# A long block model on one Trainium2 core: reordering the first mixer's projection and the start of its recurrence

## The reference, cut to what matters

```python
def project(h):
    p = h @ w_in
    qkv = jax.nn.silu(depthwise_conv(p[..., :2 * GDN_KW + GDN_VW], conv_w))
    q = _l2norm(qkv[..., :GDN_KW]...)
    k = _l2norm(qkv[..., GDN_KW:2 * GDN_KW]...)
    v = qkv[..., 2 * GDN_KW:]...
...
decay = jnp.exp(jnp.where(tril, gcum[..., :, None] - gcum[..., None, :], -jnp.inf))
lower = jnp.where(strict, jnp.einsum('nbhid,nbhjd->nbhij', kb, kc) * decay, 0.0)
sol = lax.linalg.triangular_solve(eye + lower, rhs, left_side=True, lower=True, unit_diagonal=True)
attn = jnp.where(tril, jnp.einsum('nbhid,nbhjd->nbhij', qc, kc) * decay, 0.0)
...
def step(S, inp):
    v_new = u_i - w_i @ S
    o = (q_i * exp(g_i)) @ S + a_i @ v_new
    S = S * exp(g_last) + (k_i * exp(g_last - g_i)).T @ v_new
```

## Time and profile before

| what | us |
|---|---|
| median of 3 runs | 4353.49 (4348.59 to 4356.99) |
| profiled execution, its own time | 4360.86 |
| its span | 4359.1 |
| busy: TensorE | 3892.0 (89%) |
| busy: VectorE | 1823.6 (42%) |
| busy: ScalarE | 980.9 (23%) |
| busy: GpSimd | 377.2 (9%) |

### The profile page before, as it was taken

One profiled execution on the slowest core, in us unless ns is written; L12 is line 12 of the kernel. 1 busy time (PEld: TensorE's weight loads), 2 busy tenths in 40 slices (PEclk: granted clock), 3 DMA queues, 4 the chain that ended last, 5 costly groups with the idle time before them and its releaser, 6 DMA issues.

```text
span 4359.1 us, 49807 instructions
## 1 busy us (share of the span) xinstructions
PE 3892.0 (89%) x20860; PEld 2379.2 (55%) x20860; DVE 1823.6 (42%) x2818; ACT 980.9 (23%) x1915; POOL 377.2 (9%) x928
## 2 busy tenths in 40 slices
PE   7988898898899999789888989888888999998999
PEld 4577555785534434577766765222344433445777
DVE  2644445553302212368777441110236478115443
ACT  3411223222301111345554321000124200100000
POOL 0023001210100000000000000000040077000000
PEclk9989998999899999799998998999987999999999
DMA  5232122311298897121100426999911011231331
GB/s 189 87 97 57 52 97 70 101 64 35 102 380 340 342 382 303 61 78 59 68 30 30 122 83 255 421 421 421 338 60 59 20 34 49 77 101 58 99 95 58
DMA packets 278559, 631.24 MB, mean 145 GB/s; under 512 B 63552, under 2 KB 205376, under 8 KB 219456
## 3 DMA queue, kind: packets, MB, share of 16 engines
q1 hardware_dynamic: 275712, 627.40, 39.1%
q10 hardware_dynamic: 2624, 0.66, 0.1%
HBM read 611.75 MB, written 16.25 MB: 144 GB/s over the span
## 4 chain that ended last, share of the span: by engine, by line
PE 67%; DVE 11%; DMA 10%; ACT 4%; POOL 4%; issue 2%; SPq 2%; ACTq 0%; DVEq 0%; POOLq 0%
PE ps L1505 10%; PE ps L1792 10%; PE ps L1165 6%; PE ps L1511 4%; PE ps L1842 4%; DMA arena<-moe_w_down 4%; DMA arena<-moe_w_gate 2%; PE ps L1399 2%; PE ps L1411 2%; PE ps L1658 2%; PE ps L1654 2%; PE ps L1663 2%; DMA arena<-moe_w_up 2%; PE ps L1103 2%; PE ps L2009 1%
## 5 line engine op out<-in xcount | busy, mean ns | idle before, releaser
L1505 PE MATMUL ps<-arena 128*64 128x512 f32 x3072 | 707.7, 600 | 79.6 <-DMA arena<-moe_w_up 22.4
L1505 PEld LDWEIGHTS ps<-arena 128*64 128x64 f32 x3072 | 207.3, 137 | 528.2 <-issue 383.6
L1165 PE MATMUL ps<-arena 128*128 128x512 f32 (+1 forms) x768 | 251.3, 486 | 3.5 <-DVE g_rows L2731 2.1
L3054 DVE SCALAR_TENSOR_TENSOR arena<-arena,ps 128x512 f32<-128x512 f32 (+1 forms) x48 | 30.2, 656 | 526.0 <-PE ps L1505 526.0
L3316 DVE TENSOR_TENSOR arena<-arena,ps 128x512 f32<-128x512 f32 x86 | 58.4, 687 | 444.3 <-ACT arena L2632 143.5
L1842 PE MATMUL ps<-arena 128*128 128x512 f32 x512 | 224.7, 595 | 2.9 <-issue 2.2
L1658 PE MATMUL ps<-h_first,w_rest 128*128 128x512 f32 (+1 forms) x576 | 213.8, 387 | 0.5 <-DVE arena L3213 0.5
L1165 PEld LDWEIGHTS ps<-arena 128*128 128x128 f32 x768 | 145.6, 190 | 106.1 <-issue 94.0
L1654 PE MATMUL ps<-h_second,w_rest 128*128 128x512 f32 (+1 forms) x576 | 199.6, 361 | 0.7 <-DVE h_second L3120 0.7
L3062 DVE TENSOR_TENSOR m_yx_rest<-ps,m_yx_lead 64x512 fp32r<-64x512 f32 x64 | 44.1, 689 | 361.0 <-ACT m_yc_lead L2352 206.0
L2352 ACT ACTIVATE m_yx_lead<-ps 64x512 fp32r<-64x512 f32 x64 | 37.9, 592 | 659.6 <-PE ps L1505 658.8
(11 more groups left out here) (493 smaller groups left out, 7171.7 us busy)
## 6 DMA issues: line engine op xcount, KB each, us to landing
arena<-moe_w_gate SPq DMA_DIRECT2D x128, 1024.0 KB, 9.0
arena<-moe_w_up SPq DMA_DIRECT2D x128, 1024.0 KB, 9.5
arena<-moe_w_down SPq DMA_DIRECT2D x128, 1024.0 KB, 11.1
arena<-ada_w SPq DMA_DIRECT2D x48, 1024.0 KB, 4.8
arena<-ffn_w_gate_up SPq DMA_DIRECT2D x22, 1024.0 KB, 5.0
arena<-gdn_w_in SPq DMA_DIRECT2D x16, 1024.0 KB, 9.1
arena<-w_in SPq DMA_DIRECT2D x30, 512.0 KB, 3.8
arena<-ssd_w_x SPq DMA_DIRECT2D x8, 1024.0 KB, 4.8
```

The lines of the kernel that those rows point to most:

```text
L1165: mm = pe.matmul(ps[:, 2 * (i % 2) + j, 0:nn], state.w[:, k, m * P:(m + 1) * P], hT[:, k, c0:c0 + nn], start=(k == 0), stop=(k == KD - 1))
L1505: mm = pe.matmul(ps[CAPX * h:CAPX * h + CAPX, bank, :], x[:, 0:CAPX], w[:, 512 * h:512 * h + 512], **flags)
```

## The change

Three things, in both halves.

- The order of the projected parts becomes keys, queries, values (`PARTS`), in the weight plan, on ScalarE and on VectorE.
- Pair 0 is prepared inside the projection's last tiles. TensorE does `decays(0, u)` between the two column sets of tile 10 and `scores(0, u)` between those of tile 11. VectorE makes the table of pair 0 behind tile 8, its mask and product behind tile 9, its scores behind the convolution of tile 10. ScalarE makes its exponentials behind the last root. `project` is now called from within `recurrence`.
- In SP's queue pair 0's `low_blocks` moves ahead of the last load of the gap's chunks (`GAP_LATE`), which is issued between the reads of the blocks and the scatter. SP waits for the last silu before it loads `rU` and `rT` of pair 0. VectorE makes the table of pair 1 after it has waited for that silu.

```diff
+PARTS = (1, 0, 2)
...
-                plan += [("gin", i // 4, hg, (i // 2) % 2)]
+                plan += [("gin", PARTS[i // 4], hg, (i // 2) % 2)]
...
+        GAP_LATE = [[x for x in sum(ADA[ADA_GAP[hg]:ADA_GAP[hg] + 3], []) if PLACE[x][1] >= USED[("gin", PARTS[-1], hg, 1)]] for hg in range(GH // HG)]
...
+                    if p == 0:
+                        for item in GAP_LATE[hg]:
+                            load(item)
                     sp.wait_ge(s.r_el, n + 1)
...
                     sp.wait_ge(s.r_low, LOW_DMAS * n + 416 + LOW_BASE)
+                    if p == 0:
+                        sp.wait_ge(s.gp_act, 24 * hg + 24)
...
-                    if item == FIRST_OUT[hg]:
+                    if item == (GAP_LATE[hg] + FIRST_OUT[hg:hg + 1])[0]:
                         low_blocks(hg)
...
                     for j, (c0, nn, _) in enumerate((XSET, CSET)):
+                        if j and between:
+                            between()
...
+                def keys_first():
+
+                    pe.wait_ge(s.gp_rt, 2 * (8 * hg + 8))
+                    pe.wait_ge(s.ada_copied, ADA_GAP[hg])
+                    for u in range(2):
+                        decays(0, u)
+
+                def queries_first():
+                    pe.wait_ge(s.gp_norm, 8 * hg + 8)
+                    for u in range(2):
+                        scores(0, u)
...
-                    tile(i)
+                    tile(i, {10: keys_first, 11: queries_first}.get(i))
...
-                pe.wait_ge(s.ada_copied, ADA_GAP[hg])
+                project(hg, decays, scores)
+                pe.wait_ge(s.gp_pre, 24 * hg + 24)
+                for u in units:
+                    decays(1, u)
+                for u in units:
+                    scores(1, u)
                 pe.wait_ge(s.gp_act, 24 * hg + 24)
-                pe.wait_ge(s.gp_norm, 8 * hg + 8)
-                for p in range(2):
-                    for u in units:
-                        decays(p, u)
-                    for u in units:
-                        scores(p, u)
...
+                    if i == 9:
+                        for u in range(2):
+                            decays(0, u)
...
+                    if 8 <= i < 11:
+                        first[i - 8]()
...
+                def decays_first():
+                    if hg:
+                        dve.wait_ge(s.spilled, 16)
+                    for u in units:
+                        masked(0, u)
+                    for u in units:
+                        decayed(0, u)
+
+                def queries_first():
+                    for u in units:
+                        scores(0, u)
+
+                project(hg, (lambda: table_ahead(0), decays_first, queries_first))
                 dve.wait_ge(s.gp_act, 24 * hg + 24)
```

More of the change, by code:

```diff
@@ L900, in _ @@
                     sp.dma_start(A["spill"], RT).then_inc(s.spilled, 16)
-                if item not in sum(EARLY, []):
+                if item not in sum(EARLY + GAP_LATE, []):
                     load(item)
@@ L1152, in _, with project, tile @@
             gdn_tail()
-            def project(hg):
-                def tile(i):
+            def project(hg, decays, scores):
+                def tile(i, between=None):
                     if i % 2 == 0:
-                        state.w = take(("gin", i // 4, hg, (i // 2) % 2))
+                        state.w = take(("gin", PARTS[i // 4], hg, (i // 2) % 2))
                     if i >= 2:
@@ L1418, in _ @@
             for hg in range(GH // HG):
-                project(hg)
                 recurrence(hg)
@@ L2188, in gdn_scalars, with project @@
                 a.do(act.activation(rows0[:, 512:768], ps[:, 5, 0:256], ACT.Copy), s.tl_rows)
-            def project(hg):
+            def project(hg, decays):
                 for i in range(14):
@@ L2193, in project @@
                         if i % 2:
-                            act.wait_ge(s.w_used, USED[("gin", i // 4, hg, (i // 2) % 2)])
+                            act.wait_ge(s.w_used, USED[("gin", PARTS[i // 4], hg, (i // 2) % 2)])
                         else:
@@ L2207, in project @@
                         t = i - 1
-                        dst = qkv[t // 4][:, t % 4, :]
+                        dst = qkv[PARTS[t // 4]][:, t % 4, :]
                         act.wait_ge(s.gp_conv, 12 * hg + t + 1)
@@ L2239, in decays @@
                              s.r_d if j == HG - 1 else None)
-                for p in range(2):
-                    for u in units:
-                        decays(p, u)
+                project(hg, decays)
+                for u in units:
+                    decays(1, u)
                 for b in range(ADA_GAP[hg], ADA_GAP[hg] + 3):
@@ L2734, in gdn_scalars, with project @@
                 v.do(dve.tensor_tensor(beg, beg, beta, ALU.mult))
-            def project(hg):
+            def project(hg, first):
                 for p in pre:
@@ L2744, in project @@
                     if i < 12:
-                        ch = (i // 4) * 8 + hg * HG + i % 4
+                        ch = PARTS[i // 4] * 8 + hg * HG + i % 4
                         dve.wait_ge(s.gp_pre, 2 * (12 * hg + i + 1))
@@ L2763, in project @@
                         r = rt[t % 2]
-                        dst = qkv[t // 4][:, t % 4, :]
+                        dst = qkv[PARTS[t // 4]][:, t % 4, :]
                         v.do(dve.reciprocal(r, r))
                         v.settle()
-                        scale = float(P) ** -0.5 if t < 4 else 1.0
+                        scale = float(P) ** -0.5 if PARTS[t // 4] == 0 else 1.0
                         v.do(dve.scalar_tensor_tensor(out=dst, in0=dst, scalar=scale, in1=r, op0=ALU.mult, op1=ALU.mult), s.gp_norm)
+                    if 8 <= i < 11:
+                        first[i - 8]()
             def bc(colap, n=P):
@@ L2875, in states @@
                     v.do(dve.tensor_tensor(S[u], S[u], g3(own(p, u) + 1), ALU.add), s.r_state)
-                table_ahead(0)
-                dve.wait_ge(s.gp_act, 24 * hg + 24)
[L2879 to L2889, removed]
+                def decays_first():
[6 more added lines that the diff above has]
+                def queries_first():
+                    for u in units:
+                        scores(0, u)
+                project(hg, (lambda: table_ahead(0), decays_first, queries_first))
+                dve.wait_ge(s.gp_act, 24 * hg + 24)
+                table_ahead(1)
+                for u in units:
+                    masked(1, u)
+                for u in units:
+                    decayed(1, u)
+                for u in units:
+                    scores(1, u)
                 v.do(dve.memset(oT, 0.0))
```

## The result

The changed kernel takes 4334.95 us in the median of 5 runs (4327.34 to 4336.13), the kernel before 4353.49 (4348.59 to 4362.39): a ratio of 0.9949, with a 95% interval of 0.9934 to 0.9965. The ratio is one of means: 22 us less, between 15 and 29, where the two medians lie 18.5 apart. Forecast were 25.5 us less.

A forecast was written before the change was run, and what follows sets the result against it. The bound was taken to be pair 0's trip through memory and GpSimd before `level_y`. Starting it 12.4 and 13.1 us sooner in the two halves sums to 25.5 us, 4353.5 to 4328.0 us; range 4316 to 4343, narrower 4322 to 4334.

The forecast's parts named there:

- The trip of pair 0: Chain from the last `rX` through SP and GpSimd to TensorE's `level_y`: 31.9 us, no slack, claimed as the bound.
- The start of the trip: Pair 0's last `rX` done at 212.2 in the first half; trip 12.4 us sooner there, 13.1 in the second.
- TensorE's arrival: TensorE ends its own work at 239.0, tables land at 244.1, so it still waits about 5 us before `level_y`.
- SP's moved load: The load issued between pair 0's reads and scatter in SP's queue; claimed free, at most 2 us.
- price nothing: Cost set for SP's moved load, since one load fits seven times into the 14 us before the scatter.
- about 2 us for each load: Delay of small transfers per weight load ahead, from pair 2's `low_in`: 14.9 us behind six loads against 3.15.
- GpSimd beside VectorE: Pair 0's inverse beside VectorE's tables: between +0.6 and -0.8 us per half, taken as 0.
- The clock: First `level_y` group of pair 0 again starts at the low clock; full clock would give 1.5 us more per half.
- pair 2's 15.02 us: TensorE's wait before pair 2, first half; claimed unchanged because SP and TensorE shift together, so the gain is kept.
- the first rival: Part lost on the way, by pair 0's late scores or clock, port and load: gain 12 to 18 us; chance 0.09.
- handed to pair 2: Rival: SP's weight loads behind pair 1 are held, pair 2's wait grows to 27, about 4352 us; chance 0.06.
- the half clock: Slower rival: half clock stays through pair 0's steps and beyond; 20 us per half costs 15, 4369 us; chance 0.04.

The follow-up runs named there:

- e3: Changed kernel, but SP waits for the last silu before writing pair 0's `rX` out, so the trip starts late; 4347.0 us, 0.9972 of the kernel before.
- e5: Changed kernel with pair 1's table made right behind pair 0's scores on VectorE, ahead of tile 11's convolution; 4330.4 us, 0.9935 of the kernel before.
- c1: The changed kernel unaltered, run a second time beside other kernels; 4334.0 us, 0.9945 of the kernel before.
- e6: Changed kernel with pair 0's scores between tiles 10 and 11 on TensorE and ahead of tile 10's convolution on VectorE; 4326.6 us, 0.9925 of the kernel before.
- e4: Changed kernel with all six loads of the gap's chunks issued ahead of pair 0's trip, as before the change; 4344.7 us, 0.9965 of the kernel before.
- e7: Changed kernel with pair 0's scores between tiles 10 and 11 and pair 1's table right behind them; 4320.9 us, 0.9916 of the kernel before.
- e8: Changed kernel with SP's six 1 MB weight loads moved from behind pair 1's trip to behind the reads of pairs 2, 3, 4; 4306.5 us, 0.9884 of before.

## Why the prediction was right

**What bounds.** The trip of pair 0 was named as what ends last before `level_y`. e3 moved the trip's start alone and `level_y` followed; e5 moved TensorE's work alone and it did not.

**The start of the trip.** The forecast had the splits of tiles 10 and 11 at 195.3 and 208.5 and the last `rX` done at 212.2. The trace has 193.9, 207.2 and 211.0, all some 1.3 us sooner because tile 10 itself started 1.5 sooner. The distances fell by 12.4 and 14.0 in the first profile and by 12.8 and 13.3 in c1, against 12.4 and 13.1 forecast. The product that TensorE needs in tile 11 was ready at 201.1, 6 us ahead of it.

**TensorE's arrival.** Forecast were about 5.4 us idle behind tile 11 and 5 us before `level_y`; the trace has 5.52 and 4.33. e6 used this slack up exactly.

**SP's moved load.** Moving it behind the reads cost nothing, as costed. What I had not weighed is what its old place would have cost the new trip: 7 to 9 us per half in e4. The step "price nothing" was right for the edit and silent on its worth. And "about 2 us for each load", read from six loads, was too small for one: from SP's first write to its first read it is 2.7 us in e3 and 6.7 in e4, so the single load ahead cost 4.0.

**GpSimd beside VectorE.** I took 0 between +0.6 and -0.8 per half. The inverse took 12.2 us instead of 12.8: one step was held (0.62 at 218.64, beside pair 1's table at 218.48), where before two tables held two. The Trainium skill's rule of the shared port ("SBUF — State Buffer", "SBUF: two separate sides") fits these rows, and in e7 those beside the two operations with two SBUF inputs. What it would cost here by the forecast, up to 1 us per half and a sum of 23.5, did not come true in the first half of the changed kernel: the convolution ended at 217.5, 0.2 us after the inverse had started, and the first copy took 0.64 us, and 0.76 in the second half, against 0.60 before. The overlap came in e7, at 1.7 us. The measured times cannot tell 23.5 from 25.5.

**The clock, and whether the gain is kept.** `level_y` of pair 0 started at the low clock again, as I had assumed: its first group took 3.78 us. But a statement failed, without harm to the sum. I said that pair 2's 15.02 us would stay; it is 9.2 and 9.8 in the first half of the two profiles. Two things changed it: `level_y` of pair 0 ran longer at the low clock by 2.4 to 3.7 us, which the wait for pair 2 takes up, and the stretch from pair 0's start to pair 2's was 81.9 and 81.2 instead of 84.1. In e1, which has only the new order of the parts, it was 82.7, and 80.9 in the second half, so the stretch varies by 2 us and more between executions without the change's moves. What I took for a clock cost on the path is hidden by pair 2's wait. That the gain is passed on is shown by the next fixed point: tile 10 of the second half comes 487.1 and 486.6 us after tile 10 of the first, against 501.3 before and 500.9 in e1, which is 14.2 and 14.7 less, where pair 0 gave 12.4 and 12.8.

**The total.** Measured 22 (15 to 29) and 24 (18 to 30) against 25.5. The median, 4335.0, lies inside the stated 4316 to 4343, but 1 us above my own narrower 4322 to 4334, and the times alone would not have told the forecast from the first rival's 12 to 18 us. The distances do: 26.4 and 26.1. The span of the profiled execution fell by 33.5, of which 26.4 are the two distances, 1.5 lie ahead of tile 10, and 5.6 elsewhere; one execution alone would have told too much. By the traces the rivals did not occur: nothing was handed to pair 2, no part was lost, and the half clock ended within pair 0's steps.

## What to carry to other kernels

A chain through memory and a slow engine that ends in front of the main engine is moved one for one by its start, so look for the earliest point at which its inputs exist, here before the values, and let the main engine make them between its own tiles. Then look at the queue: one bulk load ahead of the chain's small transfers cost it 16 of 26 us by the distances, and six of them, ahead of another pair's, held about as much time (27 us) as the whole reordering had won (22 to 24). Measure such a move as a distance between two fixed points of the trace, since single executions of the kernel before differ by as much as the effect (4345 to 4371).

## What the runs showed of the hardware that I had not expected

Small transfers pay for bulk ones ahead of them on the same queue: from the first write of `rX` to the first read back it was 2.7 us alone (e3, and pair 2 in e8), 6.7 behind 1 MB (e4) and 14.1 behind 6 MB (pair 2 of the changed kernel). Whether another queue would have spared them, no run tried. And GpSimd's steps of 0.3 us took the whole length of the VectorE operations beside them that had only SBUF operands, three in a row in e7: 0.6 us with one tile as input, 1.0 twice with two. Beside operations with an operand in PSUM they kept their 0.3. So where such a GpSimd chain lies was worth 1.7 us here.
